# Stick-breaking weights as exp(z minus an inclusive suffix sum), with single-pass suffix-sum matmuls

## The reference

```python
    def block(args):
        qblk, b = args
        qpos = offset + b * qb + jnp.arange(qb)
        z = jnp.einsum('bqhd,bkhd->bhqk', qblk, k) * scale + bias
        mask = key_idx[None, :] < qpos[:, None]
        log_1mb = jnp.where(mask, jax.nn.log_sigmoid(-z), 0.0)
        acc = lax.cumsum(log_1mb, axis=3, reverse=True) - log_1mb
        wts = jnp.where(mask, jnp.exp(jax.nn.log_sigmoid(z) + acc), 0.0)
        return jnp.einsum('bhqk,bkhd->bqhd', wts, v)
```

## Time and profile before

| | |
|---|---|
| median of 3 runs | 2354.62 us (2353.75 to 2356.7) |
| the profiled execution, its own time | 2357.5 us |
| its span | 2355.8 us |
| TensorE matmul busy | 2245.6 us (95%) |
| VectorE busy | 1122.0 us (48%) |
| ScalarE busy | 784.9 us (33%) |
| GpSimd busy | 115.3 us (5%) |
| mean granted TensorE clock | 0.978 of full |
| first matmul of `stick` to first matmul of `out_proj` | 1774.20 to 1901.79 us |

### The profile page before, as it was taken

The page is one execution under the profiler, slowest core; times in us unless marked ns, Lnnn a source line. Parts: engine busy times, 40 slices in busy tenths (PEclk is TensorE's granted clock), DMA queues, the critical chain, the costliest instruction groups (busy, mean ns, idle before and its releaser), DMA issues.

```text
span 2355.8 us, 43642 instructions
## 1 busy us (share of the span) xinstructions
PE 2245.6 (95%) x17746; PEld 2157.8 (92%) x17746; DVE 1122.0 (48%) x1673; ACT 784.9 (33%) x1064; POOL 115.3 (5%) x186
## 2 busy tenths in 40 slices
PE   7999999998889899999999999999998799999997
PEld 7999999997778799999999999999994379999996
DVE  5444433764346554444334444433667744444332
ACT  4222222352233443222223222223456533222222
POOL 2000000100112200000000000000003200000000
PEclk9999999998889999999999999999998999999998
DMA  4333333422200123333333333333323133333331
GB/s 123 96 90 89 89 90 91 117 81 55 60 9 1 45 86 98 90 89 91 89 95 92 89 89 91 93 90 89 90 81 109 45 90 90 94 93 89 92 89 52
DMA packets 352976, 195.70 MB, mean 83 GB/s; under 512 B 9903, under 2 KB 347979, under 8 KB 352873
## 3 DMA queue, kind: packets, MB, share of 16 engines
q1 hardware_dynamic: 344640, 172.36, 25.4%
q0 software_dynamic: 6064, 19.86, 2.8%
q10 hardware_dynamic: 2176, 2.15, 0.3%
HBM read 186.43 MB, written 8.04 MB: 83 GB/s over the span
## 4 chain that ended last, share of the span: by engine, by line
PE 66%; DVE 4%; ACT 3%; issue 1%; DMA 0%; POOL 0%; POOLq 0%; ACTq 0%; DVEq 0%
PE PS L1753 57%; PE PS L1861 5%; PE PS L2199 1%; PE PS L2167 0%; PE PS L2188 0%; PE PS L2040 0%; DVE skX L1602 0%; DVE Dm L1435 0%; DVE skX L1617 0%; PE PS L2151 0%; ACT skX L1020 0%; ACT skL L1029 0%; ACT skL L1028 0%; ACT skL L1026 0%; ACT skY L1023 0%
## 5 line engine op out<-in xcount | busy, mean ns | idle before, releaser
L1753 PE MATMUL PS<-hh,whi 128*128 128x260 f32 x3600 | 733.1, 285 | 7.8 <-DVE hl L1681 6.5
L1753 PE MATMUL PS<-hh,wlo 128*128 128x260 f32 x3600 | 728.3, 284 | 0.0
L1753 PE MATMUL PS<-hl,whi 128*128 128x260 f32 x3600 | 727.5, 284 | 0.0
L1121 DVE TENSOR_TENSOR wlo<-stage,whi 128x1024 fp32r<-128x1024 f32 x337 | 413.3, 1226 | 459.3 <-ACT whi L692 448.2
L1753 PEld LDWEIGHTS PS<-hh,whi 128*128 128x128 f32 x3600 | 560.0, 190 | 11.3 <-DVE hl L1681 4.8
L1753 PEld LDWEIGHTS PS<-hh,wlo 128*128 128x128 f32 x3600 | 558.0, 189 | 0.0
L1753 PEld LDWEIGHTS PS<-hl,whi 128*128 128x128 f32 x3600 | 557.1, 189 | 0.0
L692 ACT ACTIVATE whi<-stage 128x1024 fp32r<-128x1024 f32 x337 | 352.8, 1048 | 254.1 <-PE PS L1753 245.4
L1753 PE MATMUL PS<-act_h,whi 128*128 128x260 f32 x1408 | 283.9, 283 | 0.0
L1753 PE MATMUL PS<-act_h,wlo 128*128 128x260 f32 x1408 | 283.1, 282 | 0.0
L1753 PE MATMUL PS<-act_l,whi 128*128 128x260 f32 x1408 | 282.5, 282 | 0.0
(11 more groups left out here) (383 smaller groups left out, 1792.0 us busy)
## 6 DMA issues: line engine op xcount, KB each, us to landing
stage<-in_ffn_w_gate SPq DMA_DIRECT2D x88, 512.0 KB, 3.8
stage<-in_ffn_w_up SPq DMA_DIRECT2D x88, 512.0 KB, 3.8
stage<-in_ffn_w_down SPq DMA_DIRECT2D x64, 512.0 KB, 4.1
stage<-in_w_in_e SPq DMA_DIRECT2D x28, 512.0 KB, 3.7
stage<-in_ffn_w_down SPq DMA_DIRECT2D x32, 384.0 KB, 3.4
stage<-in_w_in_o SPq DMA_DIRECT2D x20, 512.0 KB, 3.9
stage<-in_w_out_e SPq DMA_DIRECT2D x8, 512.0 KB, 4.1
stage<-in_w_out_o SPq DMA_DIRECT2D x8, 512.0 KB, 4.1
```

The lines of the kernel that those rows point to most:

```text
L1121: dve.tensor_tensor(wlo[:, slot, :], stage[:, s % STAGE_SLOTS, :], whi[:, slot, :].bitcast(F32), ALU.subtract).then_inc(lo_ready, 1)
L1753: mm = pe.matmul(psum[:, half, :], w, x(k)[:, half * HALF:(half + 1) * HALF], start=first and w is hi and x is rhs_hi, stop=last and w is lo)
```

## The change

Per head of `stick`:

- Scores: a matmul of `ident_r` on `hide_r` (128 columns, float32r) is added for each key block, into the diagonal block of the scores. It adds -2^60 where a key isn't before the query, so both masks (L1602 on VectorE, L657 on GpSimd) go.
- ScalarE reads the scores once (Identity with the bias, into `skZ`). VectorE takes the minimum with 40 into `skL`, ScalarE does Exp and Ln on it, and VectorE takes the maximum of z and that: softplus, in `skS`.
- ScalarE copies `skS` to float32r (the high part, `skX[:, 1]`), VectorE subtracts it (the low part, `skX[:, 0]`).
- The suffix sums are now inclusive (`upto_r`), and they are matmuls of float32r on the high and on the low part; the later blocks are summed by TensorE itself (`ones_r`), not ahead by VectorE. That is 20 matmuls over 5120 columns in place of 7 over 2048.
- VectorE subtracts the sum from `skZ`, ScalarE takes Exp, and TensorE multiplies with the values.
- TensorE makes scores two heads ahead, and values(h-1) come directly after suffix(h).
- The samples' query rows go to DRAM and come back spread over the partitions by DMA (`load_q`), two ahead; the matmul L2159 goes. Each sample's two pages are one product and one sum of 1024 elements.

GpSimd makes the constants `hide_r`, `ident_r`, `upto_r`, `ones_r` early in the stage. The diff, without renumbered waits and semaphore names:

```diff
 GLA_TAU = 16.0
 RG_C = 8.0
 CLAMP = 80.0
+FAR = 2.0 ** 60
+STICK_CLAMP = 40.0
 LOOKAHEAD = 3
 SPLIT_SLOTS = 4
 STAGE_SLOTS = 2
...
-        kq = sb("kq", [P, WC], F32, st)
+        q_rows = nc.dram_tensor("q_rows", (TS, WC), F32, kind="Internal").ap()
+        qrow, kq = tmp[:, 0:2, 0:WC], tmp[:, 2:2 + PAGES, 0:WC]
...
-        skL = sb("skL", [P, SCORES], F32, st)
-        skX = sb("skX", [P, 2, SCORES], F32, st)
-        skY = sb("skY", [P, 3, SCORES], F32, st)
-        skR = sb("skR", [P, TP - P + TP - 2 * P], F32, st)
+        skL = prO[:, OV:OV + KC, :].rearrange("p a b -> p (a b)")[:, 0:SCORES]
+        skS = sb("skS", [P, SCORES], F32, st)
+        skX = sb("skX", [P, 2, SCORES], F32R, st)
+        skZ = sb("skZ", [P, 3, SCORES], F32, st)
...
-                pool.affine_select(out=before[:], in_=before[:], compare_op=ALU.is_gt, fill=0.0, base=0,
+                pool.affine_select(out=upto[:], in_=upto[:], compare_op=ALU.is_ge, fill=0.0, base=0,
+                                   pattern=[[-1, P]], channel_multiplier=1).then_inc(o_consts, 1)
+                pool.affine_select(out=hide[:], in_=hide[:], compare_op=ALU.is_gt, fill=-FAR, base=0,
                                    pattern=[[1, P]], channel_multiplier=-1).then_inc(o_consts, 1)
+                pool.tensor_copy(ident_r[:], ident[:]).then_inc(o_consts, 1)
+                pool.wait_ge(o_consts, CONSTS + 8)
+                pool.tensor_copy(hide_r[:], hide[:]).then_inc(o_consts, 1)
+                pool.tensor_copy(upto_r[:], upto[:]).then_inc(o_consts, 1)
+                pool.tensor_copy(ones_r[:], ones[:]).then_inc(o_consts, 1)
...
-                pool.wait_ge(v_rows, NB)
+                pool.wait_ge(v_rows, NB + 1)
+                pool.dma_start(q_rows, rowS[:, 0, :]).then_inc(q_saved, 16)
                 save(o["sbv_p"][0, 0].rearrange("(c p) h d -> p c (h d)", p=P), vtok[:])
...
+                pool.wait_ge(q_saved, 16)
+                load_q(0)
+                load_q(1)
                 for n in range(HC):
                     pool.wait_ge(sm_kq, n + 1)
                     load_pages(n + 4)
-                    pool.wait_ge(sk_w, n + 1)
-                    for at, _ in SCORE:
-                        block_w = skY[:, n % 3, at:at + P]
-                        last = pool.tensor_tensor(block_w, block_w, before[:], ALU.mult)
-                    last.then_inc(sk_mask, 1)
+                    if n + 2 < TS:
+                        load_q(n + 2)
                 for g in range(TS + 4, 2 * TS):
...
-                z = banks(0, 3)[:, 0:SCORES]
+                def scores(h):
+                    act.wait_ge(sk_z, h + 1)
+                    if h >= 3:
+                        act.wait_ge(sk_o, h - 2)
+                    act.activation(skZ[:, h % 3, :], banks(0, 3)[:, 0:SCORES], ACT.Identity, bias=sbb[:, 0, h:h + 1])\
+                       .then_inc(sk_read, 1)
                 act.preload_act_table_set(LN_EXP)
-                act.wait_ge(rg_c2, 2)
+                act.wait_ge(o_loaded, 96)
+                scores(0)
                 for h in range(HC + 2):
                     if h < HC:
-                        act.wait_ge(sk_z, h + 1)
-                        if h >= 2:
-                            act.wait_ge(sk_acc, h - 1)
-                        act.activation(skX[:, h % 2, :], z, ACT.Relu, bias=sbb[:, 0, h:h + 1])
-                        if h >= 3:
-                            act.wait_ge(sk_o, h - 2)
-                        act.activation(skY[:, h % 3, :], z, ACT.Relu, scale=-1.0, bias=sbb[:, 1, h:h + 1])
-                        if h:
-                            act.wait_ge(sk_added, h)
-                        act.activation(skL[:], z, ACT.Abs, bias=sbb[:, 0, h:h + 1]).then_inc(sk_read, 1)
-                        act.wait_ge(sk_read, h + 1)
-                        link(act.activation(skL[:], skL[:], ACT.Exp, scale=-1.0))
-                        act.activation(skL[:], skL[:], ACT.Ln, bias=1.0).then_inc(sk_ln, 1)
+                        act.wait_ge(sk_cut, h + 1)
+                        link(act.activation(skL, skL, ACT.Exp))
+                        act.activation(skL, skL, ACT.Ln, bias=1.0).then_inc(sk_ln, 1)
+                    if h + 1 < HC:
+                        scores(h + 1)
+                    if h < HC:
+                        act.wait_ge(sk_sp, h + 1)
+                        act.activation(skX[:, 1, :], skS[:], ACT.Copy).then_inc(sk_hi, 1)
                     if 1 <= h <= HC:
-                        act.wait_ge(sk_add, h)
-                        a = (h - 1) % 3
-                        act.activation(skY[:, a, :], skY[:, a, :], ACT.Exp, scale=-1.0).then_inc(sk_w, 1)
+                        n = h - 1
+                        act.wait_ge(sk_sub, n + 1)
+                        act.activation(skZ[:, n % 3, :], skZ[:, n % 3, :], ACT.Exp).then_inc(sk_w, 1)
...
-                def mask(buf, a):
-                    for at, _ in SCORE:
-                        last = dve.tensor_tensor(buf[:, a, at:at + P], buf[:, a, at:at + P], before[:], ALU.mult)
-                    return last
-                dve.wait_ge(o_consts, CONSTS + 5)
-                def add_later(n):
-                    dve.wait_ge(sk_acc, n + 1)
-                    dve.tensor_tensor(skY[:, n % 3, :], skY[:, n % 3, :], banks(3, 3)[:, 0:SCORES], ALU.add)\
-                       .then_inc(sk_add, 1)
+                def cut(h):
+                    dve.wait_ge(sk_read, h + 1)
+                    if h:
+                        dve.wait_ge(sk_sp, h)
+                    dve.tensor_scalar(skL, skZ[:, h % 3, :], STICK_CLAMP, None, ALU.min).then_inc(sk_cut, 1)
+                cut(0)
                 for h in range(HC):
-                    a = h % 2
+                    dve.wait_ge(sk_ln, h + 1)
                     if h:
-                        add_later(h - 1)
-                    dve.wait_ge(sk_ln, h + 1)
-                    link(dve.tensor_tensor(skX[:, a, :], skX[:, a, :], skL[:], ALU.add))
-                    link(mask(skX, a))
-                    x1, x2, x3 = (skX[:, a, at:at + w] for at, w in SCORE[1:])
-                    w1 = TP - P
-                    dve.tensor_copy(skR[:, w1:w1 + P], x2[:, 0:P])
-                    dve.tensor_copy(skR[:, 0:P], x1[:, 0:P])
-                    link(dve.tensor_tensor(skR[:, w1 + P:], x2[:, P:], x3, ALU.add))
-                    dve.tensor_tensor(skR[:, P:w1], x1[:, P:], skR[:, w1:], ALU.add).then_inc(sk_sp, 1)
-                    dve.tensor_tensor(skY[:, h % 3, :], skY[:, h % 3, :], skL[:], ALU.add).then_inc(sk_added, 1)
-                    dve.wait_ge(sk_added, h + 1)
+                        dve.wait_ge(sk_acc, h)
+                    dve.tensor_tensor(skS[:], skZ[:, h % 3, :], skL, ALU.max).then_inc(sk_sp, 1)
+                    if h + 1 < HC:
+                        cut(h + 1)
+                    dve.wait_ge(sk_hi, h + 1)
+                    dve.tensor_tensor(skX[:, 0, :], skS[:], skX[:, 1, :].bitcast(F32), ALU.subtract)\
+                       .then_inc(sk_lo, 1)
                     sample_scores(h)
-                add_later(HC - 1)
+                    dve.wait_ge(sk_acc, h + 1)
+                    dve.tensor_tensor(skZ[:, h % 3, :], skZ[:, h % 3, :], banks(3, 3)[:, 0:SCORES], ALU.subtract)\
+                       .then_inc(sk_sub, 1)
             def sample_scores(b):
-                dve.wait_ge(sm_q, b + 1)
+                dve.wait_ge(q_loaded[b % 2], 16 * (b // 2 + 1))
                 dve.wait_ge(page_loaded[b % 4], 16 * PAGES * (b // 4 + 1))
-                for p in range(PAGES):
-                    link(dve.tensor_tensor(kq[:], pages[:, b % 4, p, :], banks(7, 1), ALU.mult))
-                    last = dve.tensor_reduce(smS[:, 0, p, b, :], kq[:].rearrange("p (h d) -> p h d", h=HC), AX.X, ALU.add)
-                    if p < PAGES - 1:
-                        link(last)
-                last.then_inc(sm_kq, 1)
-                dve.wait_ge(sm_kq, b + 1)
+                if b:
+                    dve.wait_ge(sm_kq, b)
+                q = qrow[:, b % 2:b % 2 + 1, :].to_broadcast([P, PAGES, WC])
+                link(dve.tensor_tensor(kq, pages[:, b % 4], q, ALU.mult))
+                dve.tensor_reduce(smS[:, 0, :, b, :], kq.rearrange("p a (h d) -> p a h d", h=HC), AX.X, ALU.add)\
+                   .then_inc(sm_kq, 1)
...
-                for h in range(HC + 2):
+                pe.wait_ge(o_consts, CONSTS + 11)
+                def score(h):
+                    r = slice(h % 2 * HDC, (h % 2 + 1) * HDC)
+                    if h:
+                        pe.wait_ge(sk_read, h)
+                    for n, (at, w) in enumerate(SCORE):
+                        z = banks(0, 3)[:, at:at + w]
+                        pe.matmul(z, prO[r, OK + h // 2, n * P:(n + 1) * P], prO[r, OQ + h // 2, n * P:TP],
+                                  start=True, stop=False)
+                        mm = pe.matmul(z[:, 0:P], ident_r[:], hide_r[:], start=False, stop=True)
```

(42 more changed lines are left out.)

41 lines of the change are left out of this document (25 added, 16 removed).

## The result

Slower: 2373.26 us (median of 4, 2372.67 to 2374.3) against 2354.61 us (2353.75 to 2356.7), a ratio of 1.0074 with a 95% interval of 1.0061 to 1.0086. That is 18.7 us more where 11.0 less were forecast; 2373.3 lies far outside the range. The profiled execution took 2372.67 us, 15.2 more than that of before, which was 2.9 above its own median.

A forecast was written before the change was run, and what follows sets the result against it. TensorE was taken as busy 95%, so only `stick`'s ring of waits and TensorE's work there could yield. Last values end at 1864.75 instead of 1875.76, 11.0 us less: 2354.6 - 11.0 = 2343.6 us, range 2336.8 to 2350.8.

The forecast's parts named there:

- five rings: Middle heads of `stick`: each head takes one ring of waits, 9.10 us, up to head 6's subtraction at 1851.9.
- Clock 1.00 between 1810 and 1860: Sign that the forecast is right: TensorE's clock stays full through the middle heads of `stick`.
- rival B: Clock falls in every head of `stick` from about 1.5 us idle: 16.6 us a head, 2393 us; chance 0.06.
- The masks, 0.36 us a head: Four float32r mask matmuls of 128 columns in each head's scores on TensorE: 0.36 us, bounds 0.21 to 0.48.
- The start: First heads of `stick`: scores 0 from 1774.20, scores 2 from 1783.2, first subtraction done at 1795.2.
- The ring: Longest chain of waits per middle head: 9.10 us against 10.45 before; a second one is 9.02 us.
- Suffix sums 2.54 us: 20 float32r suffix matmuls per head on TensorE: 2.54 us, bounds 2.13 to 2.82, against 3.7 before.
- Rival A: Single-pass suffix matmuls no cheaper than the 3.7 us now: ring 10.3 us, 2353.1 us; chance 0.08.
- VectorE and ScalarE: Work per head: VectorE 7.8 us, with minimum 0.86 and sample product and sum 1.25 each; ScalarE 7.0 us.
- The query row: First sample's query row, through DRAM, lands at about 1790.5; hidden by 0.7 us behind suffix sums 0.
- rival C: Query rows land late, at 1800 instead of 1790.5: only 4.9 us gained, 2349.8 us; chance 0.08.
- The end, 26.0 us: From the last value matmuls through `samples_o` up to `out_proj`: keeps its length of 26.0 us.

The follow-up runs named there:

- run 1: Changed kernel with three spare float32 matmuls behind each head's value matmuls, filling TensorE's wait: 2360.13 us, ratio 1.002.
- run 2: Changed kernel without the four mask matmuls of each head (output left wrong in part): 2355.04 us, ratio 1.0.
- run 10: run 6 with spare matmuls where TensorE would wait at both ends of the stage: 2341.28 us, ratio 0.994.
- run 6: Changed kernel with masks grouped and values of head h-1 ahead of suffix sums of head h, ScalarE reordered likewise: 2348.37 us, ratio 0.9968.
- run 4: Changed kernel with only the order changed: values of head h-1 ahead of suffix sums of head h, ScalarE likewise: 2359.7 us, ratio 1.0018.
- run 12: Kernel before the change, with spare matmuls at both ends of its stage: 2352.18 us, ratio 0.9986.
- run 7: Changed kernel with mask matmuls over the same 64 rows as the scores (output left wrong in part): 2360.42 us, ratio 1.002.
- run 3: Changed kernel with the mask matmuls in plain float32 instead of float32r: 2377.42 us, ratio 1.0091.
- run 5: Changed kernel with the masks of key blocks 0 to 2 grouped behind their three scores, then block 3 with its mask: 2363.99 us, ratio 1.0044.

## Why the prediction was wrong

The sum by its steps, in us. The forecast's points are counted from its first score at 1774.20. The stage came out 28.0 us longer than forecast:

| step | forecast | after | run 1 |
|---|---|---|---|
| first score to end of first subtraction | 21.0 | 27.7 | 27.7 |
| to the second | 11.1 | 10.7 | 10.7 |
| five rings, to head 6 | 45.6 | 65.4 | 52.8 |
| to the last | 8.5 | 10.3 | 8.9 |
| to the end of the last values | 4.35 | 4.3 | 4.3 |
| to `out_proj` | 26.0 | 26.2 | 26.3 |
| sum | 116.6 | 144.6 | 130.7 |

- **"Clock 1.00 between 1810 and 1860"**: the step that failed most. The low clock is 12.6 of the 19.8 us that the five rings were too short (65.4 against 52.8 in run 1, whose distance per head is that of full clock), and most of the 1.8 us of the last head (10.3 against 8.9). I had rival B written out, with a chance of 0.06, and held the row from 780 against it: 3.90 of 5 us busy at clock 1.00. That row has other matmuls and idles of another pattern; it says nothing of a wait of 1.5 us in front of score matmuls. The rows from 1795 and 1801 in the same group, where the clock fell during a wait of 2.77 us in this very stage and stayed down into 1803, were the nearer ones; I had them, but for a longer wait. The same stage of before, with two waits of some 0.5 us a head, had clock 1.00 from 1806 to 1868, so between these nothing on hand told what 1.5 us would do, and 0.06 was too sure. B's own price was too high: half of a head runs slowly, not the whole. (Its 5.4 us for scores and masks at half clock was too low: 7.1 and 6.9 us.)
- **The masks, 0.36 us a head**: they cost 1.4 to 1.5 us (runs 1 and 2). I bounded them by columns and by a 260-column row in a stream of one shape, and that stream has no change of shape between matmuls. In the five rings scores and masks take 3.86 us instead of 2.72, 1.14 us a head and 5.7 of the 7.2 us that the low clock doesn't explain.
- **The start**, 6.7 us too short, is both of these. The forecast let TensorE begin the scores of head 2 at 9.0 us, which leaves some 3.6 us for those of head 1; it began them at 14.0, because the scores and masks of head 1 ran at half clock and took 7.1 us. Those of head 2 took 6.9 us instead of 5.4.
- **The ring** that decides is not the first one (scores copy, float32r copy, low part, suffix sums, values; 9.10 us) but the second (scores copy, scores, suffix sums, values; 9.02 us). They stood 0.08 us apart, and the dear masks lie in the second alone: 10.56 us at full clock. The mask-free run 2 has the first, at 9.49 us: 0.3 us by the suffix sums, the rest at handovers.
- **Suffix sums 2.54 us**: 2.85 us at full clock until the values begin, at the upper bound (2.82), which is 0.3 us a head or 1.5 us of the five rings. Rival A fell: single pass is cheaper than the 3.7 us of before. Stands.
- **VectorE and ScalarE**: minimum 0.83, product and sum 1.23 and 1.22, subtraction 1.49, copies 1.26 to 1.33 us. Stands.
- **The query row**, forecast 16.3 us after the first score, came after 17.6, and VectorE waited 0.89 us for it, behind suffix sums that ended later still. Hidden, as forecast, but by the slow clock; in run 10 it is the bound of the start, the case that rival C describes.
- **The end, 26.0 us**: 26.2. Stands.

## What to carry to other kernels

When an edit takes work from TensorE in a stage where it is nearly the bound, price the stage at both clocks and give the low one a real chance: ask where the wait will now lie and reorder so that the engine's own queue covers it (run 6; the order alone, run 4, was not enough). Count the changes of shape in a stream of matmuls, not only their columns, and group equal ones. Compare a mended version with the old kernel given the same mending (run 12), or the gain is put down to the wrong edit; and look whether the mending took hold there, since in run 12 spare matmuls at half clock cost time at the start.

## What the runs showed of the hardware

- A change between matmuls of 64 and 128 rows costs some 0.14 to 0.18 us (runs 1, 6 and 7).
- The clock fell with TensorE busy for over 10 us without a gap (run 4), and stayed up with a wait of 0.33 us in 8.84 (run 6) and with two of some 0.5 us in 10.45 (before). With a wait of 1.48 us in each head it fell in some heads (run 2) or in each (after, runs 3, 5 and 7). What decides isn't settled. Neither waits nor changes of shape do alone: runs 1 and 4 have the same score groups and no wait, and only in run 4 did it fall; run 7 has no change of shape in its score groups, and it fell. Run 6 differs from run 4 in fewer changes of shape and in a short wait, and no run tells these apart.
- float32r matmuls of 128 columns follow each other in 0.11 us at full clock (the last two suffix matmuls start at 1822.29 and 1822.40) and in 0.21 us at half clock (1797.85 and 1798.06). The Trainium skill (TensorE: Matmul & The Clock Gate, section LDWEIGHTS) has about 107 ns for a load of 128 weight columns; this agrees at full clock.
